# The sum of the two expert rows of row tiles 1 to 4 on GpSimd instead of VectorE

## The chip, the cores and the metric

The kernel runs on one core of a Trainium2 chip. The metric is the device time of one launch in microseconds (us); three runs of the kernel before gave 1686.21 to 1688.44, with a median of 1687.64. A core has TensorE (PE), VectorE (DVE), ScalarE (ACT), GpSimd (POOL) and SyncE (SP). All of them issue work in program order from a queue of their own, and wait for one another on semaphores. PE, DVE, ACT and POOL compute; here POOL and SP also issue the transfers between HBM and the on-chip memory (SBUF).

## The reference

A step of a two-layer (DEPTH = 2) transformer over 640 rows of 1024 numbers: 128 rows of a prompt and 512 latent rows. Each layer has attention and then a mixture of experts:

```python
sh1, sc1, gt1, sh2, sc2, gt2 = modulation(cond, lp['w_mod'], lp['b_mod'])
h = rms_norm(x, lp['g_norm1']) * (1 + sc1) + sh1
... # attention on h @ w_in, two branches, then
x = x + gt1 * mixed
h2 = rms_norm(x, lp['g_norm2']) * (1 + sc2) + sh2
x = x + gt2 * moe(h2, lp['w_router'], lp['b_router'], lp['w_gate'], lp['w_up'], lp['w_down'])
```

The mixture picks two experts for each row and adds their two outputs, each times its weight. What the change touches is the last line: the two weighted expert outputs of a row are added, multiplied by the gate `gt2` and added to `x`; and, in the next layer, the first line of the norm reads that `x`.

## The kernel before

The 640 rows are five row tiles of 128 (t = 0 is the prompt). All arithmetic is fp32; the large products are made of three passes over values that are split in a high and a low part (`hi`, `lo`). The engines' programs are written out by hand, in the order in which they run, with a semaphore (`Signal`) for each hand-over.

The mixture works on 18 tiles of gathered rows. Its outputs are scattered to a buffer in HBM (`ye_d`), the first and the second expert's row of each token in two halves. When the last tile has been stored, SP loads them back (`load_back`, L605 to L610): for each row tile t, `Y1[t]` and `Y2[t]`, 128 x 1024 fp32 or 512 KB each, and signals `gathered[t]`. The old `x` and the gate `gt` have been brought back earlier (`rows_return`, L590 to L601). Then VectorE does three operations for each row tile: the sum of the two rows (`mix_rows`, L1355), the gate (`gate_rows`, L1359) and the addition to `x` (`add_rows`, L1363), which signals `x_ready[t]`.

This happens at two places.

- **The change of layers**, at the start of layer 1. VectorE does row tile 0, and then in its loop over t: the mean square of tile t, the inverse root (L1319 to L1325), the three operations of tile t+1, half of the normed and modulated tile t read from PSUM (`head_half`, L1335), and the low part of it (`head_lo`, L1344). ScalarE squares `x` (`head_square`, L952), takes the root (L956), scales the row tile (`head_xn`, L960), and reads the other half from PSUM (`head_evac`, L966 to L972). TensorE transposes the scaled tile (L1800) in the middle of the projection of the tile before it (L1882 to L1884). `qk_evac` (L985, L986) takes the finished projection of a tile to SBUF, and VectorE sums its squares (`head_sum`, L1349).
- **The tail**, after layer 1: nothing is left but the five row tiles, three operations each, and SP stores each finished tile to `y_out` (L669).

GpSimd computes nothing in the kernel before. It issues transfers: in the mixture the indirect ones (rows of `xg`, weights of the experts, the stores to `ye_d`, L827), and at the change of layers one copy of `x` to HBM (L716), when `x_ready` of the last row tile has come.

Of the kernel before, what the change touches and what calls it, by code (L numbers as in the profile page):

```python
# [18 lines left out]
ALU = mybir.AluOpType  # L19
# [7 lines left out]
DEPTH = 2  # L27
NT = 5
# [109 lines left out]
def program(nc, w_stream, w_gu, w_dn, x_in, c_cols, params, b_mod2, vecs, g_norm2, da_kc, da_vc, na_kc, na_vc, na_bias,  # L138
# [3 lines left out]
    with ctx:  # L142
# [3 lines left out]
        def at(name, shape, dt, kb=None):  # L146

            size = int(np.prod(shape[1:])) * (2 if dt == BF16 else 4)
            if kb is None:
                off = top[0]  # L150
                top[0] += (size + 31) // 32 * 32
            else:
                off = area + int(kb * 1024)
                assert int(kb * 1024) + size <= AREA_KB * 1024, name
            return nc.alloc_sbuf_tensor_at(name, shape, dt, offset=off)

        def sem(name):
            return ctx.enter_context(nc.semaphore(name))
# [32 lines left out]
        tri = at("tri", [P, P], BF16)  # L191
# [71 lines left out]
        tri_f = at("tri_f", [P, P], F32, 48)  # L263
        x = at("x", [P, NT, D], F32, 0)
        gt = at("gt", [P, 2, D], F32, 20)
        Y1 = [at(f"y1_{t}", [P, D], F32, kb) for t, kb in enumerate((36, 74, 78, 82, 86))]
        Y2 = [at(f"y2_{t}", [P, D], F32, 50 + 4 * t) for t in range(NT)]
# [103 lines left out]
        s_zero = sem("zeros_ready")  # L371
# [1 line left out]
        s_cond = sem("cond_loaded")  # L373
        p_loaded = [sem(f"p_loaded{i}") for i in range(KC // 2)]
        p_used = sem("p_used")
        s_tri = sem("tri_cast")
        s_modini = sem("mod_bias")

        dve_chain = Signal("dve_chain", 0)
# [98 lines left out]
        y_dve = Signal("y_dve", MOE_TILES)  # L478
        y_stored = [Signal(f"y_stored{b}", half[b], 0, 16) for b in range(2)]
        gathered = [Signal(f"gathered{t}", 5 if t == 0 else 3, 0, 16) for t in range(NT)]  # L480
        x_ready = Signal("x_ready", NT)


# [190 lines left out]
        def _(po):  # L674
# [17 lines left out]
            for l in range(DEPTH):  # L692
# [11 lines left out]
                def load_vec(dst, which, cond, s):  # L704
                    po.dma_start(dst, mod_d[l, cond, which * D:(which + 1) * D].partition_broadcast(P)).then_inc(s.sem, 16)

                def norm_vecs():
# [3 lines left out]
                    for cond in range(2):  # L711
                        load_vec(sh[:, cond, :], 3, cond, shift_loaded)

                if l >= 1:
                    po.wait_ge(x_ready.sem, x_ready.at(l - 1, NT - 1))
                    po.dma_start(x_spill, x[:]).then_inc(x_spilled.sem, 16)  # L716

# [106 lines left out]
                def store_rows(n):  # L824
                    po.wait_ge(y_act.sem, y_act.at(l, n))
                    po.wait_ge(y_dve.sem, y_dve.at(l, n))
                    po.indirect_dma_start(ye_d, bass.IndirectOffsetOnAxis(row_i[:, XD_COL[n]:XD_COL[n] + 1], 0),  # L827
                                          ysb[n % 2][:], None, bounds_check=2 * NT * P - 1,
                                          oob_is_err=False).then_inc(y_stored[n % 2].sem, 16)
# [38 lines left out]
                store_rows(MOE_TILES - 2)  # L868
                store_rows(MOE_TILES - 1)

            po.wait_ge(x_parked.sem, x_parked.layer * DEPTH)
            for s in (kv_out, mod_stored, h2_stored, y_stored[0], y_stored[1], sg_stored[0], sg_stored[1]):
                po.wait_ge(s.sem, s.layer * DEPTH)
# [334 lines left out]
        def _(dve):  # L1208
# [4 lines left out]
            dve.wait_ge(s_const, 128)  # L1213
            dve.tensor_copy(rc[:], rc_f[:])
            dve.tensor_scalar(br_b[:], br_b[:], 0.5, None, ALU.add)
            dve.tensor_copy(tri[:], tri_f[:]).then_inc(s_tri, 1)
            steps = count()
            for l in range(DEPTH):

# [4 lines left out]
                def chained(ins):  # L1224
                    ins.then_inc(dve_chain.sem, 1)
                    return step()

                def after(n):
                    dve.wait_ge(dve_chain.sem, dve_chain.at(0, n))
# [121 lines left out]
                                      AX.X, ALU.add).then_inc(sum_ready.sem, 1)  # L1351

                def mix_rows(l, t):
                    dve.wait_ge(gathered[t].sem, gathered[t].at(l, gathered[t].n - 1))
                    after(chained(dve.tensor_tensor(Y1[t][:], Y1[t][:], Y2[t][:], ALU.add)))  # L1355

                def gate_rows(l, t):
                    mix_rows(l, t)
                    return chained(dve.tensor_tensor(Y1[t][:], Y1[t][:], gt[:, GI(t), :], ALU.mult))  # L1359
# [105 lines left out]
                for i in range(len(DA_UNITS) + 3):  # L1465
                    if 1 <= i <= len(DA_UNITS):
                        j = i - 1
                        t, h = DA_UNITS[j]
# [26 lines left out]
                    if i >= 3 and DA_UNITS[i - 3][1] == DA_HEADS - 1:  # L1495
                        t = DA_UNITS[i - 3][0]
# [290 lines left out]
        def _(pe):  # L1787
            def keep_busy(n, bank):
                for _ in range(n):
                    pe.matmul(ps[:, bank, 0:4 * HD], ident[:], rope_c[:].rearrange("p a b -> p (a b)"), start=True, stop=True)  # L1790
# [32 lines left out]
            keep_busy(2, 2)  # L1823
            head_columns(0)
            keep_busy(11, 2)
            pe.wait_ge(s_tri, 1)
            for l in range(DEPTH):

                def mod_pair(g, kc):
# [571 lines left out]
```

## Time and profile before

| | |
|---|---|
| three runs, median (lowest to highest) | 1687.64 us (1686.21 to 1688.44) |
| the profiled execution, own time | 1685.31 us |
| its span | 1683.5 us |
| PE busy | 1552.3 us, 92% |
| DVE busy | 899.7 us, 53% |
| ACT busy | 701.3 us, 42% |
| POOL busy | 296.0 us, 18% |

The span is what the records of the trace cover, the own time also what lies around it (1.8 us). Busy shares are means over stages with different limits. The change acts on two short stretches, 847 to 907 us and 1657 to 1683.5 us of the span, so those are read by themselves, in order of time.

### The profile page before, as it was taken

The page shows a single profiled execution, that of the slowest core. Times are in us where ns is not written, and L with a number is a line of the kernel's source. Part 1 is how long each engine was busy: PE and PEld are TensorE (multiplying, and loading weights), DVE is VectorE, ACT ScalarE, POOL GpSimd, SP SyncE. Part 2 cuts the span into 40 slices and gives each one's busy share as a digit, 9 for nine tenths or more (in the row PEclk, how much of TensorE's full clock was granted, in tenths as well). Part 3 has the DMA queues.
Part 4 walks back from the last instruction along what each step waited for, and adds up shares of the span by engine and source line. Part 5 has one row for each costly group of instructions (what it writes and reads, how often), then busy time and mean ns, then how long its engine had stood idle before and what let it go on. Part 6 is the DMA issues. An engine that isn't in the chain of part 4 may idle for free.

```text
span 1683.5 us, 21787 instructions
## 1 busy us (share of the span) xinstructions
PE 1552.3 (92%) x8180; PEld 1107.9 (66%) x8180; DVE 899.7 (53%) x1723; ACT 701.3 (42%) x1335; POOL 296.0 (18%) x321
## 2 busy tenths in 40 slices
PE   4999999999999989798869999999999999889992
PEld 1777777777787854454547777777778878555561
DVE  1576664445554744344575756553465556344554
ACT  4543554445522314344554455534554132134550
POOL 1000000011101015454200010000111010355540
PEclk9999999999999989999989999999999999999996
DMA  8541206534366289989635512354345253898747
GB/s 339 206 145 63 69 26 204 177 111 155 126 216 265 86 321 411 419 321 377 219 150 190 193 50 70 112 180 140 113 151 196 92 200 125 325 416 355 272 144 286
DMA packets 92376, 337.55 MB, mean 201 GB/s; under 512 B 20960, under 2 KB 21024, under 8 KB 89328
## 3 DMA queue, kind: packets, MB, share of 16 engines
q1 hardware_dynamic: 53136, 197.68, 32.3%
q0 software_dynamic: 38992, 135.86, 21.5%
q10 hardware_dynamic: 144, 2.62, 0.4%
q8 instruction: 65, 1.06, 0.3%
q14 instruction: 39, 0.32, 0.1%
HBM read 351.22 MB, written 47.35 MB: 237 GB/s over the span
## 4 chain that ended last, share of the span: by engine, by line
PE 82%; DMA 8%; DVE 5%; ACT 2%; issue 1%; SPq 1%; POOL 0%; POOLq 0%; ACTq 0%; DVEq 0%
PE ps L1882 17%; PE ps L1884 17%; PE ps L1883 17%; DMA dn_b<-w_dn,eidx 6%; PE ps L1874 5%; PE ps L2212 5%; PE ps L2261 4%; PE ps L2034 3%; PE ps L2016 2%; PE ps L1841 2%; PE ps L2094 2%; PE ps L2228 2%; PE ps L1790 1%; PE ps L2195 1%; PE ps L2068 1%
## 5 line engine op out<-in xcount | busy, mean ns | idle before, releaser
L1882 PE MATMUL ps<-hi,hT_hi 128*128 128x512 f32 x960 | 392.9, 409 | 5.5 <-ACT o_a L1092 3.0
L1884 PE MATMUL ps<-hi,hT_lo 128*128 128x512 f32 x960 | 376.8, 393 | 0.0
L1883 PE MATMUL ps<-lo,hT_hi 128*128 128x512 f32 x960 | 376.5, 392 | 0.0
L1882 PEld LDWEIGHTS ps<-hi,hT_hi 128*128 128x128 f32 x960 | 182.3, 190 | 63.8 <-issue 20.3
L1884 PEld LDWEIGHTS ps<-hi,hT_lo 128*128 128x128 f32 x960 | 181.3, 189 | 40.0
L1883 PEld LDWEIGHTS ps<-lo,hT_hi 128*128 128x128 f32 x960 | 182.2, 190 | 32.5
L888 ACT ACTIVATE hi<-raw 128x1024 fp32r<-128x1024 f32 x106 | 108.6, 1055 | 136.6 <-DMA raw<-w_stream 136.6
L1234 DVE TENSOR_TENSOR lo<-raw,hi 128x1024 fp32r<-128x1024 f32 x106 | 127.4, 1221 | 63.8 <-ACT hi L888 63.5
L1713 DVE TENSOR_TENSOR lo<-raw,hi 128x1024 fp32r<-128x1024 f32 x96 | 112.8, 1222 | 39.1 <-ACT hi L1159 39.1
L2212 PE MATMUL ps<-gu_a,xT 128*64 128x512 f32 x256 | 113.3, 595 | 0.0
L2212 PE MATMUL ps<-gu_b,xT 128*64 128x512 f32 x256 | 113.3, 595 | 0.0
L1159 ACT ACTIVATE hi<-raw 128x1024 fp32r<-128x1024 f32 x96 | 95.5, 1056 | 5.0 <-PE ps L1884 5.0
L2261 PE MATMUL ps<-dn_a,hidT 128*64 128x512 f32 x128 | 65.2, 657 | 24.9 <-DMA dn_b<-w_dn,eidx 23.3
L1069 ACT ACTIVATE e_da<-ps,neg_m 128x640 f32<-128x640 f32 (+1 forms) x80 | 56.0, 705 | 71.5 <-DVE neg_m L1491 71.4
L1491 DVE TENSOR_REDUCE neg_m<-ps 128x1 f32<-128x640 f32 (+1 forms) x80 | 53.7, 713 | 56.7 <-PE ps L2023 38.1
L1756 DVE TENSOR_TENSOR hid<-ps,silu_g 128x256 f32<-128x256 f32 x36 | 15.3, 425 | 118.0 <-ACT silu_g L1185 102.1
L2212 PEld LDWEIGHTS ps<-gu_a,xT 128*64 128x64 f32 x256 | 33.7, 137 | 66.7 <-issue 66.7
L1349 DVE TENSOR_REDUCE ssum<-sq 128x8 f32<-128x512 f32 x40 | 27.3, 685 | 79.2 <-ACT stg L986 79.2
L1176 ACT ACTIVATE ysb<-ps,w_slot 128x512 f32<-128x512 f32 x36 | 24.8, 689 | 107.6 <-PE ps L2261 61.5
L1730 DVE TENSOR_SCALAR ysb<-ps,w_slot 128x512 f32<-128x512 f32 x36 | 27.0, 751 | 77.8 <-PE ps L2261 43.4
L985 ACT ACTIVATE sq<-ps 128x512 f32<-128x512 f32 x40 | 24.0, 599 | 105.8 <-PE ps L1884 105.8
L1185 ACT ACTIVATE silu_g<-ps 128x256 f32<-128x256 f32 x36 | 13.8, 384 | 124.5 <-PE ps L1884 61.4
(312 smaller groups left out, 2917.6 us busy)
## 6 DMA issues: line engine op xcount, KB each, us to landing
raw<-w_stream SPq DMA_DIRECT2D x112, 512.0 KB
raw<-w_gu SPq DMA_DIRECT2D x80, 512.0 KB
raw_m<-w_stream SPq DMA_DIRECT2D x68, 512.0 KB, 5.6
raw<-w_dn SPq DMA_DIRECT2D x40, 512.0 KB
bias_na<-na_bias POOLq DMA_DIRECT2D x32, 384.0 KB, 3.3
sg<-sg_d POOLq DMA_DIRECT2D x8, 1280.0 KB, 9.1
y<-ye_d SPq DMA_DIRECT2D x20, 512.0 KB, 7.3
raw_p<-w_stream SPq DMA_DIRECT2D x16, 512.0 KB, 16.3
```

The lines of the kernel that those rows point to most:

```text
L888: act.activation(hi[s][:], raw[s][:], ACT.Copy).then_inc(is_hi.sem, 1)
L1069: act.activation(e_da[:, i % 2, m, 0:nk], ps_flat[:, m * 1024:m * 1024 + nk], ACT.Exp, bias=neg_m[:, 2 * (i % 2) + m:2 * (i % 2) + m + 1], ...
L1159: act.activation(hi[k][:], raw[w][:], ACT.Copy).then_inc(is_hi.sem, 1)
L1234: dve.tensor_tensor(lo[s][:], raw[s][:], hi[s][:].bitcast(F32), ALU.subtract).then_inc(is_lo.sem, 1)
L1491: dve.tensor_reduce(neg_m[:, c:c + 1], ps_flat[:, m * 1024:m * 1024 + nk], AX.X, ALU.max, negate=True).then_inc(mx_done.sem, 1)
L1713: dve.tensor_tensor(lo[w][:], raw[w][:], hi[k][:].bitcast(F32), ALU.subtract).then_inc(is_lo.sem, 1)
L1874: ins = pe.transpose(ps[:, 5 + n % 2, j * P:(j + 1) * P], src, ident[:])
L1882: pe.matmul(out, w_hi, m_hi, start=first, stop=False)
L1883: pe.matmul(out, w_hi, m_lo, start=False, stop=False)
L1884: return pe.matmul(out, w_lo, m_hi, start=False, stop=last)
L2212: ins = pe.matmul(ps[cs, 0, :], xT[:, kc, cs], pair_gu[q % 2][h][:, kc * 512:(kc + 1) * 512], start=(kc == 0), stop=(kc == KC - 1))
L2261: ins = pe.matmul(ps[cs, 2 + c, :], hidT[:, k, cs], pair_dn[q % 2][h][k][:, c * 512:(c + 1) * 512], start=(k == 0), stop=(k == 1))
```

## The change

GpSimd gets `sum_rows`, which waits for `gathered[t]` and adds `Y2[t]` to `Y1[t]` for t = 1 to 4; it stands ahead of its copy of `x` at the change of layers, and at the end of its program for the tail. VectorE's `mix_rows` keeps the sum of row tile 0, and for the others waits for GpSimd's signal `y_summed` and goes on with the gate and `x`. To have a semaphore for it, `s_tri` is given up, and the wait of TensorE for it at the start becomes a wait for the third count of `s_zero`, raised by the same instruction.

```diff
+        y_summed = Signal("y_summed", NT - 1)
...
+                def sum_rows(l):
+                    for t in range(1, NT):
+                        po.wait_ge(gathered[t].sem, gathered[t].at(l, gathered[t].n - 1))
+                        po.tensor_tensor(Y1[t][:], Y1[t][:], Y2[t][:], ALU.add).then_inc(y_summed.sem, 1)
+
                 if l >= 1:
+                    sum_rows(l - 1)
                     po.wait_ge(x_ready.sem, x_ready.at(l - 1, NT - 1))
                     po.dma_start(x_spill, x[:]).then_inc(x_spilled.sem, 16)
...
+            sum_rows(DEPTH - 1)
             po.wait_ge(x_parked.sem, x_parked.layer * DEPTH)
...
-            dve.tensor_copy(tri[:], tri_f[:]).then_inc(s_tri, 1)
+            dve.tensor_copy(tri[:], tri_f[:]).then_inc(s_zero, 1)
...
                 def mix_rows(l, t):
+                    if t >= 1:
+                        dve.wait_ge(y_summed.sem, y_summed.at(l, t - 1))
+                        return
                     dve.wait_ge(gathered[t].sem, gathered[t].at(l, gathered[t].n - 1))
                     after(chained(dve.tensor_tensor(Y1[t][:], Y1[t][:], Y2[t][:], ALU.add)))
...
-            pe.wait_ge(s_tri, 1)
+            pe.wait_ge(s_zero, 3)
```

Line numbers differ in the changed kernel: the sum, the gate and the addition to `x` on VectorE are L1365, L1369 and L1373 there, the sum on GpSimd is L717, the copy of `x` L722, the store to `ye_d` L833. GpSimd's queue at the change of layers, before (`y_1_152` is `Y1[1]`, `y_1_157` is `Y2[1]`):

```order
L827 DMA ye_d<-ysb_251,row_i 1280x1024
L827 DMA ye_d<-ysb_93,row_i 1280x1024
L716 DMA x_spill<-x 128x5120
L721 DMA kT<-da_kc 128x4x128
L722 DMA v<-da_vc 128x512
```

and GpSimd's queue at the same place now:

```order
L833 DMA ye_d<-ysb_251,row_i 1280x1024
L833 DMA ye_d<-ysb_93,row_i 1280x1024
L717 ISA
L717 TENSOR_TENSOR y_1_152<-y_1_152,y_1_157 128x1024
L717 TENSOR_TENSOR y_2_153<-y_2_153,y_2_158 128x1024
L717 TENSOR_TENSOR y_3_154<-y_3_154,y_3_159 128x1024
L717 TENSOR_TENSOR y_4_155<-y_4_155,y_4_160 128x1024
L722 DMA x_spill<-x 128x5120
```

Four sums stand ahead of the copy of `x`, and in front of the first of them an instruction `ISA` without operands, which the build adds and which waits for nothing. The tail's four sums have no such row.

VectorE's queue at the change of layers, before, from the end of the last split of weights:

```order
L1238 TENSOR_TENSOR lo_65<-raw_64,hi_66 128x1024
L1355 TENSOR_TENSOR y_0_151<-y_0_151,y_0_156 128x1024
L1359 TENSOR_TENSOR y_0_151<-y_0_151,gt 128x1024
L1363 TENSOR_TENSOR x<-x,y_0_151 128x1024
L1313 TENSOR_SCALAR nv<-xss 128x1
L1319 RECIPROCAL n_114<-n_114 128x1
L1320 SCALAR_TENSOR_TENSOR nr<-n_114,nv 128x1
L1322 TENSOR_SCALAR nr<-nr 128x1
L1325 TENSOR_TENSOR nr<-nr,n_114 128x1
L1355 TENSOR_TENSOR y_1_152<-y_1_152,y_1_157 128x1024
L1359 TENSOR_TENSOR y_1_152<-y_1_152,gt 128x1024
L1363 TENSOR_TENSOR x<-x,y_1_152 128x1024
```

and VectorE's queue there now, from the inverse root of row tile 0:

```order
L1326 RECIPROCAL n_114<-n_114 128x1
L1327 SCALAR_TENSOR_TENSOR nr<-n_114,nv 128x1
L1329 TENSOR_SCALAR nr<-nr 128x1
L1332 TENSOR_TENSOR nr<-nr,n_114 128x1
L1369 TENSOR_TENSOR y_1_152<-y_1_152,gt 128x1024
L1373 TENSOR_TENSOR x<-x,y_1_152 128x1024
L1342 TENSOR_SCALAR y_0_151<-ps,mT 128x128 x4
L1351 TENSOR_TENSOR hT_lo<-y_0_151,hT_hi 128x4x128 x2
```

Each of the row tiles 1 to 4 has lost its first 128 x 1024 operation on VectorE; everything else stands in the order of before. In the tail the same four operations are gone from VectorE's 15.

## Rows read from the trace of the kernel before

**Rows 1.** Timeline of DVE, change of layers: start us, us, engine, line, op [idle <-releaser]

```profile
847.54 1.23 DVE L1355 TENSOR_TENSOR y<-y,y 128x1024 f32<-128x1024 f32 x1 [2.55 <-DMA y<-ye_d]
...
850.06 1.23 DVE L1363 TENSOR_TENSOR x<-x,y 128x1024 f32<-128x1024 f32 x1
...
853.18 0.22 DVE L1320 SCALAR_TENSOR_TENSOR nr<-n,nv 128x1 f32<-128x1 f32 x1
...
853.70 1.22 DVE L1355 TENSOR_TENSOR y<-y,y 128x1024 f32<-128x1024 f32 x1
...
856.21 1.23 DVE L1363 TENSOR_TENSOR x<-x,y 128x1024 f32<-128x1024 f32 x1
857.35 1.36 DVE L1335 TENSOR_SCALAR y<-ps,mT 128x128 f32<-128x128 f32 x4
...
865.25 1.36 DVE L1335 TENSOR_SCALAR y<-ps,mT 128x128 f32<-128x128 f32 x4
```

**Rows 2.** Timeline of ACT, change of layers

```profile
853.82 1.15 ACT L960 ACTIVATE y<-x,nr 128x1024 f32<-128x1024 f32 x1 [0.87 <-DVE nr L1325]
...
858.75 0.63 ACT L972 ACTIVATE hT_hi<-y 128x512 fp32r<-128x512 f32 x1 [0.87 <-DVE y L1335]
859.28 1.04 ACT L952 ACTIVATE y<-x 128x1024 f32<-128x1024 f32 x1
...
868.64 0.58 ACT L985 ACTIVATE sq<-ps 128x512 f32<-128x512 f32 x1
```

**Rows 3.** Timeline of PE, change of layers

```profile
860.15 0.50 PE L1882 MATMUL ps<-hi,hT_hi 128*128 128x512 f32 x1 [1.88 <-DVE hT_lo L1344]
...
862.91 1.09 PE L1800 MATMUL ps<-ident,y 128*128 128x128 f32 x8 [1.08 <-ACT y L960]
```

**Rows 4.** Chain that ended last, one turn of it: start us, us, what

```profile
879.24 0.60 ACT sq L985
...
880.35 0.69 DVE ssum L1349
...
882.99 1.97 PE ps L1800 x8
...
889.84 0.60 ACT sq L985
```

**Rows 5.** Timeline of DVE and of SP's queue, tail

```profile
1662.14 1.22 DVE L1355 TENSOR_TENSOR y<-y,y 128x1024 f32<-128x1024 f32 x1 [7.88 <-DMA y<-ye_d]
...
1665.91 14.95 SPq L669 DMA_DIRECT2D y_out<-x  x5
...
1679.28 1.23 DVE L1363 TENSOR_TENSOR x<-x,y 128x1024 f32<-128x1024 f32 x1
```

**Rows 6.** Line L610, issue and landing of the ten loads: change of layers

```profile
L610 SPq DMA_DIRECT2D y<-ye_d x10: 326/444/807, 842.7 to 847.3; - x10
...
DMA to landing us min/median/max: 3.4/7.3/11.1
```

**Rows 7.** The same line in the tail

```profile
L610 SPq DMA_DIRECT2D y<-ye_d x10: 319/446/809, 1657.3 to 1662.0; - x10
...
DMA to landing us min/median/max: 3.5/7.3/12.6
```

**Rows 8.** Timeline of POOL, last store, and three issues within the mixture

```profile
840.53 0.97 POOL L827 DMA_INDIRECT ye_d<-ysb,row_i  x1 [4.33 <-DVE ysb L1730]
...
1604.85 1.00 POOL L792 DMA_INDIRECT xg<-h_d,inv_i  x1 [3.37 <-PE ps L2195]
1606.16 1.67 POOL L801 DMA_INDIRECT gu_b<-w_gu,eidx  x1 [0.30 <-issue]
...
1612.06 1.95 POOL L808 DMA_INDIRECT dn_a<-w_dn,eidx  x1 [0.31 <-issue]
```

**Rows 9.** Timeline of DVE around those three issues

```profile
1605.74 1.23 DVE L1713 TENSOR_TENSOR lo<-raw,hi 128x1024 fp32r<-128x1024 f32 x1 [1.66 <-ACT hi L1159]
...
1609.64 5.77 DVE L1713 TENSOR_TENSOR lo<-raw,hi 128x1024 fp32r<-128x1024 f32 x5 [0.52 <-ACT hi L1159]
```

**Rows 10.** All of line L1713: duration ns min/median/max, first and last start us

```profile
L1713 DVE TENSOR_TENSOR lo<-raw,hi x96: 1217/1220/1227, 644.6 to 1640.6; 128x1024 fp32r<-128x1024 f32 x96
```

More of the change, by code:

```diff
@@ L375, in program @@
         p_used = sem("p_used")
-        s_tri = sem("tri_cast")
         s_modini = sem("mod_bias")
```

## The prediction

> **What bounds the kernel now.** I read the page first: TensorE is busy for 92% of the span and makes most of the chain, so an operation taken from VectorE can only pay where TensorE waits. Then I read, in order of time, the two stretches in which VectorE's row operations stand: the change of layers and the tail.
>
> At the change of layers the loads of the expert rows end the wait at 847.54, and VectorE does the three operations of row tile 0, the last from 850.06 to 851.3 [rows 1]. ScalarE squares it, VectorE makes the inverse root (L1320 at 853.18), ScalarE scales the tile at 853.82 [rows 1, 2]. VectorE then does the three operations of row tile 1, at a spacing of 1.26 us, from 853.70 to 857.4, and only then reads row tile 0 back from PSUM, at 857.35, though the transposes had long been done; ScalarE's L972 waits 0.87 us for that and its square of tile 1 follows at 859.28; TensorE starts its projection at 860.15 after a wait for VectorE's L1344 [rows 1 to 3]. The transposes of tile 1 come at 862.91 [rows 3], and the first projection is taken out at 868.64 [rows 2]. From here on the chain turns once in 10.6 us (879.24 to 889.84): the evacuation, the small sum L1349, the scaling, the transposes, three units of matmuls [rows 4]. None of VectorE's row operations is in that turn. So VectorE's operations bound something for row tiles 0 and 1 only.
>
> In the tail VectorE is alone: first operation at 1662.14, last one ending at 1680.5, then one store [rows 5]. Fifteen operations, five tiles of 1.26 + 1.26 + 1.14 = 3.66 us.
>
> **When the data come.** The ten loads are issued by 847.3, and the slowest lands 11.1 us after its issue, so the last row tile is there at 858.4; the first is there at 847.5. Between them lie four tiles, 2.7 us each: tiles 1 to 4 at about 850.2, 853, 855.7, 858.4 [rows 1, 6]. In the tail the last one is at 1662.0 + 12.6 = 1674.6 and the first at 1662.1, so 3.1 us each at most: I take 1665.2, 1668.3, 1671.5, 1674.6 [rows 5, 7].
>
> **What a sum costs on GpSimd.** No row shows GpSimd computing. Below, it can be no faster than VectorE with the same shape, 1.22 us [rows 1]. ScalarE reads one operand of this shape in 1.15 us [rows 2]; two read one after the other make 2.30, and a third pass for the result 3.45, the upper end. I take 2.30 us: it is the plain case of an engine that takes its two operands in turn, and it lies in the middle of the bounds. The Trainium skill's page "GPSIMD Engine Reference" (section 3.1) gives 4497 ns for 2048 fp32 numbers and says that the two inputs share one read port; by it the sum would be near 2.3 us as well. No row here shows it.
>
> **Do the two engines disturb each other?** This decides the sign. In the mixture GpSimd's issue of an indirect transfer takes 1.00 us at 1604.85, when VectorE is idle. At 1606.16 it takes 1.67 us; VectorE's L1713, two operands from SBUF, runs until 1606.97. At 1612.06 it takes 1.95 us, within five such operations back to back [rows 8, 9]. So GpSimd is held up by 0.7 to 0.95 us, about until the running operation of VectorE ends, and then gets on although a further one is queued. VectorE's L1713 shows nothing of it: 96 of them within 1217 to 1227 ns [rows 10]. One direction is thus seen, with a GpSimd instruction that touches little memory; the other, VectorE held up by a GpSimd instruction that reads two whole tiles, has no row. Bounds: nothing, or the whole length of the GpSimd sum for each VectorE operation with two SBUF operands that meets one. I take the second, since the rows show a wait of whole operations and not a slight slowing.
>
> The rule that speaks against this change is in the Trainium skill, page "SBUF — State Buffer", section "Who interferes with whom": a VectorE instruction with two SBUF inputs and a GpSimd instruction that reads SBUF exclude each other, and the second to issue blocks until the first is done. Rows 8 and 9 agree with it for VectorE first and GpSimd second. By that rule all four sums and all of VectorE's row operations have to run one after the other, as in my forecast; without it the first rival holds.
>
> **The tail, with exclusion.** VectorE ends row tile 0 at 1665.9. From there 4 sums x 2.30 = 9.2 us and 4 x (1.26 + 1.14) = 9.6 us of gates and additions share one door, in whatever order: end at 1684.7 instead of 1680.5. The stores and the landings (last at 1674.6) do not bind. **+4.2 us.**
>
> **The change of layers, with exclusion.** Sum 1 has its data at about 850.2 to 851 and gets in after the addition of tile 0: 851.3 to 853.6. L1320 (two operands) waits from 853.18 to 853.6; sum 2 gets in behind it, 853.7 to 856.0, and L1325 waits for it, so the scaling of tile 0 starts at 856.3 instead of 853.82: 2.5 us late. Now it matters who goes first when both wait. If they alternate: sum 3 until 858.4, gate 1 until 859.6, sum 4 until 862.0, addition 1 until 863.2, and L1335 starts there instead of at 857.35, 5.9 late. If VectorE goes on: gate and addition of tile 1 until 858.7, L1335 is 1.4 us late, but sum 3 and sum 4 then meet L1344 and the inverse root of tile 1, and the transposes of tile 1 come 3.6 us late instead. Behind that the shorter queue for tile 2 gives 0.6 us back (the take-out at 868.64 waited for ScalarE, which was held by L1335 at 865.25 [rows 1, 2]). That makes +5.3 or +3.0; I take the middle, **+4.1 us**. From there on the turn of rows 4 passes it on unchanged.
>
> **The rest.** The removed operations themselves: 1.26 us x 4 at each place, already counted. GpSimd's queue: behind the four sums stands only the copy of `x`, which waits for the last `x_ready` anyhow; its sums are done by then. In the tail nothing stands behind them but final waits. The `ISA` row before the first sum waits for nothing, and GpSimd is free from 841.5 [rows 8] until the first data at 850 to 851: up to 9 us of it are hidden, at nothing; above that each us delays tile 1. The Trainium skill's "GPSIMD Engine Reference" (section 2.1) speaks of about 6 us for the first call of newly loaded code; by it the row would be hidden, and no row here shows one. The semaphore change at the start raises the same count by the same instruction: nothing.
>
> **Sum.** 4.2 + 4.1 = +8.3 us. The profiled execution took 1685.31 us (1683.5 of span and 1.8 around it), so 1693.6 on its scale. It lies 2.3 us under the median of the three runs; on the median's scale that is 1695.9. I say 1695.5.
>
> **The rivals.**
>
> 1. *VectorE is not held up.* Then L1335 of tile 0 needs no third operation before it and starts 1.1 to 1.2 us earlier, ScalarE's L972 and the square of tile 1 follow 0.9 earlier, and for tile 1 ScalarE is ready before the matmuls end, so that the take-out of 868.64 comes 1.7 us earlier. In the tail the last tile is 1674.6 + 2.3 + 0.1 + 2.4 = 1679.4 instead of 1680.5: 1.1 less. Together -2.8 us, 1684.8 by the median. For it: VectorE's constant 1.22 us in rows 10. Against it: GpSimd's stretched issues. Even here the gain of 16 us of VectorE's work is mostly not to be had, because tiles 2 to 4 hang on another chain. Chance 0.25.
> 2. *They share more finely, or the sum holds the door for less than it lasts.* With 1.22 to 1.7 us for each sum, the tail comes to -0.1 to +1.8 and the change of layers to 0 to +1.4: together within -0.1 and +3.2, 1687.5 to 1690.8. For it: an issue that waits still gets on at the next boundary, with VectorE unslowed. Chance 0.15.
> 3. *The sum takes the upper end, 3.45 us, or the `ISA` row lasts well over 9 us.* At 3.45 us, 4 x 1.15 more in the tail (+8.8) and twice as many lost at the change of layers (+7 to +10): about +17, 1705. Against it: it needs three separate passes. Chance 0.05.
> 4. *The change of layers gains nothing and loses nothing, because something else ends that stretch.* Speaking against it: the trace has a wait of TensorE for VectorE there, 1.88 us [rows 3]. It would leave +4.2. I count it with the forecast.
>
> **How the numbers follow.** Forecast (exclusion, 2 to 2.5 us per sum, +6 to +10): 0.55. Its own range is 1693 to 1698.5. What a measurement can tell from no change is about 0.2% of the time, 3.4 us. Rival 1 lies within that (-2.8), with a small chance of more: if GpSimd took 1.7 us, the tail would gain 1.6 and the sum be -3.4. Faster by over 0.2%: 0.04. Within: 0.21 of rival 1 and most of rival 2, with little of the forecast: 0.35. Slower by over 0.2%: 0.61. The range that holds 8 in 10 has to take in most of rival 1 on the one side and alternation at every meeting on the other: 1684.8 to 1699.5.
>
> **What would show it.** In the changed profile: GpSimd rows L717 of about 2.3 us, eight of them; if exclusion holds, VectorE's L1369 and L1373 either last over 2 us or start late beside a sum, L1332 of row tile 0 ends near 856, and the last L1373 ends about 22 us after the first L1365 of the tail, where it was 18.4. If L1369 and L1373 keep 1.22 us beside the sums, rival 1 has won. A steady 10.6 us turn for row tiles 2 to 4 shows that nothing was to be won there. What would make the forecast wrong: a sum much shorter than 2 us, or VectorE unhindered.

## The result and the profile after

The changed kernel takes 1692.77 us (median of 14 runs, 1687.81 to 1697.04), the kernel before 1686.53 us (14 runs, 1682.18 to 1690.92). The ratio is 1.0033, with a 95% interval of 1.0023 to 1.0044: +5.6 us (3.9 to 7.4). The whole interval lies above 1, so the changed kernel is slower, by a third of a per cent. The forecast was 1695.5 us, from a sum of +8.3.

The page of the profile after, its span and its busy times:

```profile
span 1691.6 us, 21789 instructions
...
PE 1555.1 (92%) x8180; PEld 1109.7 (66%) x8180; DVE 901.5 (53%) x1715; ACT 700.5 (41%) x1335; POOL 318.9 (19%) x329
```

VectorE has eight instructions of 1.22 us fewer (1715; it had 1723) and is busy for 901.5 us where it was 899.7. The work is gone and the busy time is not. The trace books the time for which an instruction is held as part of its duration, so the page hides what happened; the timelines show it.

GpSimd's sums, first the groups of line L717 in the changed kernel (duration ns min/median/max, first and last start), then its timeline at the two places (start us, us, engine, line, op, idle before and releaser); they answer to [rows 8]:

```profile
L717 POOL TENSOR_TENSOR y<-y,y x8: 2327/3008/3397, 852.1 to 1678.2; 128x1024 f32<-128x1024 f32 x8
L717 POOLq MODIFY_POOL_CONFIG  x2: 39/39/39, 841.4 to 841.4; - x2
```

```profile
852.09 11.71 POOL L717 TENSOR_TENSOR y<-y,y 128x1024 f32<-128x1024 f32 x4 [10.70 <-DMA y<-ye_d]
...
1669.83 11.64 POOL L717 TENSOR_TENSOR y<-y,y 128x1024 f32<-128x1024 f32 x4 [9.07 <-DMA y<-ye_d]
```

An undisturbed sum takes 2.33 us, and two of the eight do. The other six take 2.76 to 3.40, because GpSimd too waits, for the operation that VectorE is in. The `ISA` row of the order appears as an instruction of 39 ns at 841.4, and the first sum waits for its data until 852.09, so nothing of it is on the path.

VectorE at the change of layers, in the changed kernel (answers to [rows 1]):

```profile
848.89 1.23 DVE L1365 TENSOR_TENSOR y<-y,y 128x1024 f32<-128x1024 f32 x1 [2.79 <-DMA y<-ye_d]
...
853.91 0.15 DVE L1320 TENSOR_SCALAR nv<-xss 128x1 f32<-128x1 f32 x1 [1.28 <-ACT y L959]
...
854.53 0.34 DVE L1327 SCALAR_TENSOR_TENSOR nr<-n,nv 128x1 f32<-128x1 f32 x1
...
855.09 2.08 DVE L1332 TENSOR_TENSOR nr<-nr,n 128x1 f32<-128x1 f32 x1
857.09 1.21 DVE L1369 TENSOR_TENSOR y<-y,gt 128x1024 f32<-128x1024 f32 x1
858.34 3.26 DVE L1373 TENSOR_TENSOR x<-x,y 128x1024 f32<-128x1024 f32 x1
861.52 1.35 DVE L1342 TENSOR_SCALAR y<-ps,mT 128x128 f32<-128x128 f32 x4
862.79 2.16 DVE L1351 TENSOR_TENSOR hT_lo<-y,hT_hi 128x512 fp32r<-128x512 f32 x2
```

L1332 works on one number per partition. It takes 0.16 us alone and 2.08 here, beside the second sum. L1373 takes 3.26 instead of 1.22, beside the third. L1369 between them runs free. L1342 starts 12.63 us after the first row operation, where it was 9.81 [rows 1]. That is +2.82, and the rows give it: 1.92 + 2.04 us of holding and 0.12 at L1327 make 4.08, less 1.26 for the sum that VectorE no longer does.

The fourth sum (860.47 to 863.80) falls on L1342 and L1351. L1342 keeps its time. L1351, which has two SBUF operands, lasts 2.16 us for its two halves; in the kernel before it was

```profile
858.62 1.48 DVE L1344 TENSOR_TENSOR hT_lo<-y,hT_hi 128x512 fp32r<-128x512 f32 x2
```

That is another 0.7 us of holding, and TensorE waits for this operation (answers to [rows 3]):

```profile
865.01 0.50 PE L1892 MATMUL ps<-hi,hT_hi 128*128 128x512 f32 x1 [1.67 <-DVE hT_lo L1351]
...
867.33 1.09 PE L1810 MATMUL ps<-ident,y 128*128 128x128 f32 x8 [0.65 <-ACT y L967]
```

Counted from VectorE's first row operation, the first projection starts 3.5 us late (16.12 against 12.61) and the transposes of row tile 1 start 3.1 us late (18.44 against 15.37).

ScalarE in the changed kernel, the scaling of row tile 0 and the first take-out of a projection (answers to [rows 2]):

```profile
857.20 1.15 ACT L967 ACTIVATE y<-x,nr 128x1024 f32<-128x1024 f32 x1 [2.90 <-DVE nr L1332]
...
872.58 0.60 ACT L992 ACTIVATE sq<-ps 128x512 f32<-128x512 f32 x1 [0.40 <-PE ps L1894]
```

From VectorE's first row operation to the scaling it is 8.31 us, before 6.28. To the take-out it is 23.69, before 21.10 [rows 1, 2]: +2.6.

VectorE in the tail of the changed kernel (answers to [rows 5]):

```profile
1666.67 1.22 DVE L1365 TENSOR_TENSOR y<-y,y 128x1024 f32<-128x1024 f32 x1 [7.74 <-DMA y<-ye_d]
...
1672.64 3.35 DVE L1369 TENSOR_TENSOR y<-y,gt 128x1024 f32<-128x1024 f32 x1 [2.23 <-POOL y L717]
1676.02 3.25 DVE L1373 TENSOR_TENSOR x<-x,y 128x1024 f32<-128x1024 f32 x1
1679.19 3.36 DVE L1369 TENSOR_TENSOR y<-y,gt 128x1024 f32<-128x1024 f32 x1
1682.58 1.22 DVE L1373 TENSOR_TENSOR x<-x,y 128x1024 f32<-128x1024 f32 x1
...
1687.38 1.23 DVE L1373 TENSOR_TENSOR x<-x,y 128x1024 f32<-128x1024 f32 x1
```

Sum, operation, sum, operation: VectorE and GpSimd take turns. The tail lasts 21.94 us from the first start to the last end and lasted 18.37 [rows 5], +3.6. The parts: a wait of 2.23 for the first sum, three operations held by some 2.1 each (6.3), less four removed sums of 1.25 (5.0).

The two profiled spans differ by 8.1 us. Start to the first row operation +1.35 (848.89 against 847.54), take-out of row tile 3 at the change of layers +1.0, the unchanged code between the two places +2.2, the tail +3.6, the end equal. So the two places account for 4.6, and 3.5 are differences of stretches that the edit doesn't touch.

### The profile page after: what moved, and what is told of

It is laid out like the page before. It is cut to its first block, busy times and chain, and to the rows that moved or that the text cites. A ratio compares the mean times of both kernels' runs of the same rounds, so it can differ in the third digit from the quotient of the medians.

```text
span 1691.6 us, 21789 instructions
## 1 busy us (share of the span) xinstructions
PE 1555.1 (92%) x8180; PEld 1109.7 (66%) x8180; DVE 901.5 (53%) x1715; ACT 700.5 (41%) x1335; POOL 318.9 (19%) x329
## 4 chain that ended last, share of the span: by engine, by line
PE 81%; DMA 10%; DVE 5%; ACT 1%; issue 1%; SPq 1%; POOL 0%; POOLq 0%; ACTq 0%; DVEq 0%
PE ps L1892 17%; PE ps L1894 16%; PE ps L1893 16%; DMA dn_b<-w_dn,eidx 6%; PE ps L1884 5%; PE ps L2222 5%; PE ps L2271 4%; PE ps L2044 3%; PE ps L2026 2%; PE ps L1851 2%; PE ps L1800 2%; PE ps L2104 2%; PE ps L2238 2%; DMA raw_m<-w_stream 2%; PE ps L2205 1%
## 5 line engine op out<-in xcount | busy, mean ns | idle before, releaser
L2271 PE MATMUL ps<-dn_b,hidT 128*64 128x512 f32 x128 | 66.3, 667 | 0.0
```

The lines of the kernel that those rows point to most:

```text
L2271: ins = pe.matmul(ps[cs, 2 + c, :], hidT[:, k, cs], pair_dn[q % 2][h][k][:, c * 512:(c + 1) * 512], start=(k == 0), stop=(k == 1))
```

## Where the change of layers gives back 1.6 us

The first take-out is 2.6 us late, the fourth only 1.0. The chain of waits of the changed kernel, in order of time (start us, us, what), holds the turn of [rows 4] twice, with different lengths:

```profile
872.58 0.60 ACT sq L992
...
876.33 1.97 PE ps L1810 x8
878.30 0.43 PE ps L1892
...
883.06 0.60 ACT sq L992
...
886.81 1.09 PE ps L1810 x8
887.90 0.23 PE ps L1892
...
892.04 0.60 ACT sq L992
```

The turn from 872.58 takes 10.48 us, the next one 8.98. The difference is TensorE's clock. Busy time by stretch (stretch, us, busy us and count of PE, PEld, DVE, ACT, POOL; then the granted clock, DMA share, GB/s), of the changed kernel and then of the kernel before:

```profile
876.00:879.00 3.00, 2.67 (x11) 2.48 (x12) 2.12 (x5) 1.78 (x5) 0.00 (x0) 0.51 0.00 0
879.30:896.30 17.00, 12.15 (x59) 9.58 (x58) 9.64 (x24) 10.59 (x20) 0.61 (x1) 0.99 0.36 154
```

```profile
872.80:876.20 3.40, 3.40 (x13) 2.92 (x11) 3.37 (x7) 2.24 (x6) 0.00 (x0) 0.50 0.00 0
876.20:883.00 6.80, 4.37 (x20) 3.26 (x19) 3.82 (x10) 4.01 (x7) 0.00 (x0) 1.00 0.00 0
883.00:886.40 3.40, 3.40 (x12) 3.08 (x13) 3.37 (x6) 2.14 (x5) 0.60 (x1) 0.50 0.00 0
```

A granted clock of 0.50 is TensorE's lower level, 1.2 GHz, 1.0 the upper, 2.4 GHz. Before, TensorE pauses at the start of each turn, and the transposes behind the pause run at the lower level (0.50 from 872.80 to 876.20, and again from 883.00 to 886.40): 1.97 us for the eight of them, 0.43 us for a step of the chain behind them, a turn of 10.6. In the changed kernel one of three turns keeps the upper level through its transposes: 1.09 and 0.23, 8.98 in all. Its pause is as long as that of the turn before it, 2.43 us each, so the length of the pause doesn't tell the two apart. A delay at the start of this stretch thus isn't passed on one to one. Which turns are spared differs from kernel to kernel and, as `ride_copy` shows below, also where the code of this stretch is the same. The cause of that choice stays open.

## The experiments

The theory was the forecast's: a VectorE operation with two SBUF operands and a GpSimd instruction that reads SBUF exclude each other. The rivals: GpSimd's sums delay through their results alone (VectorE waits for them), or only certain sums matter. In the kernels that move sums to GpSimd, `ON_POOL` lists their row tiles by layer (tiles 1 to 4 in both would be the changed kernel), and the rest of the edit is this:

```diff
+                    for t in ON_POOL[l]:
+                        po.wait_ge(gathered[t].sem, gathered[t].at(l, gathered[t].n - 1))
+                        po.tensor_tensor(Y1[t][:], Y1[t][:], Y2[t][:], ALU.add).then_inc(y_summed.sem, 1)
...
+                    if t in ON_POOL[l]:
+                        dve.wait_ge(y_summed.sem, len(ON_POOL[0]) * l + ON_POOL[l].index(t) + 1)
+                        return
```

### The tail alone

```diff
+ON_POOL = {0: (), 1: (1, 2, 3, 4)}
```

> GpSimd's sums are kept in the tail alone; the change of layers is as in the kernel before. Theory A (the two engines exclude each other while GpSimd sums): from the start of VectorE's first row operation of the tail to the end of its last one 21.9 us, as in the changed kernel, against 18.4 before; +3.5 us, ratio about 1.002. VectorE's operations beside a sum last 2 to 3.4 us. Theory B (no exclusion, VectorE only waits for the sum of its row tile and the sum is slow): VectorE keeps 1.22 us per operation and the stretch is at most 0.5 us off 18.4. If the loss of the changed kernel sits in the change of layers alone, this one is level with the kernel before.

Measured: 1689.24 us (12 runs), ratio 1.0019 (1.0006 to 1.0033), that is +3.2 us (1.0 to 5.6). The tail lasts 21.94 us in its profile, as in the changed kernel, and the take-outs at the change of layers stand within 0.2 us of where they stood before (21.10, 31.70, 42.32 and 52.91 us after the first row operation). The tail is the larger and the steadier part of the loss.

### The change of layers alone

```diff
+ON_POOL = {0: (1, 2, 3, 4), 1: ()}
```

> GpSimd's sums are kept at the change of layers alone; the tail is as in the kernel before. Theory A: the first projection is taken out (ScalarE's square of it) 23.7 us after VectorE's first row operation, against 21.1 before: +2.6 us; the last one +1 to +2.6, the difference being turns in which TensorE keeps its full clock at the transposes; ratio 1.0005 to 1.0015. Together with the run that keeps the tail's sums it adds up to the changed kernel's 1.0033. Theory B: 1.7 us less than before at the first take-out, ratio 0.999.

Measured: 1688.62 us (12 runs), ratio 1.0010 (0.9997 to 1.0023), +1.7 us (-0.5 to +3.9). VectorE reads row tile 0 from PSUM 12.63 us after its first row operation, exactly as in the changed kernel. The first take-out is 2.6 us late (23.68) and the fourth 0.7 us early (52.05), since two turns of this profile are of the short kind; the expectation had it 1 to 2.6 us late. By the time alone this part can't be told from nothing; that the start of the stretch is late is read from the profile. The two parts, +0.19% and +0.10%, make up the whole, +0.33%, within their intervals.

### GpSimd reads a tile twice for nobody

The kernel before, with four sums into buffers that nobody reads, when the rows of a tile have landed. VectorE does all its own work and waits for none of them.

```diff
+            spare = [G[:, 0, :], G[:, 1, :]] + [r[:].rearrange("p a b -> p (a b)") for r in raw_h[1]]
+            for t in range(1, NT):
+                po.wait_ge(gathered[t].sem, gathered[t].at(DEPTH - 1, gathered[t].n - 1))
+                po.tensor_tensor(spare[t - 1], Y2[t][:], Y2[t][:], ALU.add)
```

> The kernel before, with VectorE's fifteen tail operations unchanged; beside them GpSimd does four additions of two 128x1024 operands into spare memory, each when the loads of row tile 1 to 4 have landed. VectorE waits for none of them. Theory A: each addition holds VectorE for its 2.3 us whenever both want to run, so the tail stretch grows from 18.4 to 25 to 27.6 us, and single operations of VectorE last up to 3.4 us. Theory B: 18.4 us, since nothing waits for GpSimd.

Measured: one run, 1692.39 us. The tail of its profile lasts 24.90 us, +6.5. Timeline of GpSimd, and of VectorE:

```profile
1665.50 5.51 POOL L874 TENSOR_TENSOR G<-y 128x1024 f32<-128x1024 f32 x2 [8.88 <-DMA y<-ye_d]
```

```profile
1665.21 1.22 DVE L1367 TENSOR_TENSOR x<-x,y 128x1024 f32<-128x1024 f32 x1
1666.36 2.91 DVE L1359 TENSOR_TENSOR y<-y,y 128x1024 f32<-128x1024 f32 x1
1669.30 2.80 DVE L1363 TENSOR_TENSOR y<-y,gt 128x1024 f32<-128x1024 f32 x1
```

Four operations of VectorE last 2.80 to 2.91 us and the eleven others 1.22 or 1.23. Nothing waits for a result here, so this settles the mechanism: GpSimd's instruction itself holds VectorE, one operation per sum, by 1.6 to 1.7 us. The expectation had 2.3 us for each and 25 to 27.6 us for the tail. The sum is shorter when both operands are the same tile: the second one here ends 1.7 us after the VectorE operation for which it waited (1671.01 against 1669.27). In the changed kernel it is 2.2 us, from 1675.99, the end of L1369, to the end of this one:

```profile
1674.87 3.32 POOL L717 TENSOR_TENSOR y<-y,y 128x1024 f32<-128x1024 f32 x1
```

### GpSimd reads one tile for nobody

```diff
-                po.tensor_tensor(spare[t - 1], Y2[t][:], Y2[t][:], ALU.add)
+                po.tensor_copy(spare[t - 1], Y2[t][:])
```

> As the kernel before, with four GpSimd copies of one 128x1024 operand into spare memory beside VectorE's tail, at the landing of row tiles 1 to 4; nothing waits for them. If any GpSimd instruction that reads from SBUF excludes VectorE's two-operand operations, the tail stretch grows by the length of the four copies (1 to 3.5 us each; 4 to 14 us in all). If only GpSimd's second read stream does, it stays at 18.4 us.

Measured: one run, 1692.42 us; the tail lasts 21.59 us, +3.2. Timeline of GpSimd, and of VectorE:

```profile
1669.56 1.07 POOL L874 COPY G<-y 128x1024 f32<-128x1024 f32 x1 [9.60 <-DMA y<-ye_d]
1672.03 1.84 POOL L874 COPY G<-y 128x1024 f32<-128x1024 f32 x1 [1.40 <-DMA y<-ye_d]
```

```profile
1669.65 2.06 DVE L1359 TENSOR_TENSOR y<-y,y 128x1024 f32<-128x1024 f32 x1
1671.74 1.23 DVE L1363 TENSOR_TENSOR y<-y,gt 128x1024 f32<-128x1024 f32 x1
1673.00 1.94 DVE L1367 TENSOR_TENSOR x<-x,y 128x1024 f32<-128x1024 f32 x1
```

One read stream is enough. The copy at 1669.56 holds the VectorE operation that starts 0.09 us after it by 0.84 us. The copy at 1672.03 meets one that began at 1671.74, waits for it itself (1.84 instead of 1.07 us) and then holds the next one. Four copies, four held operations of 1.94 to 2.06 us.

This run also shows how much of a single time comes from the turns. Its code at the change of layers is that of before, and its first take-out comes 23.18 us after the first row operation instead of 21.10, beside a stretch from 861.4 to 868.3 in which the granted clock is 0.51 (1.00 in the kernel before). That is 2.1 us without any edit there. The +3.2 of the tail is read from the tail; the single time is not used.

### GpSimd writes one tile for nobody

```diff
-                po.tensor_copy(spare[t - 1], Y2[t][:])
+                po.memset(spare[t - 1], 0.0)
```

> As the kernel before, with four GpSimd fills (128x1024, write only) of spare memory beside VectorE's tail, at the landing of row tiles 1 to 4. If it is reading that excludes, the tail stretch stays at 18.4 us and no operation of VectorE lasts over 1.3 us. If any use of SBUF by GpSimd excludes, it grows by the length of the fills, about 1 us each.

Measured: one run, 1689.87 us; the tail lasts 18.35 us, as before (18.37). A row of GpSimd, and the VectorE operation that starts 0.10 us before it with the one behind:

```profile
1669.33 0.95 POOL L874 MEMSET G<- 128x1024 f32 x1 [8.61 <-DMA y<-ye_d]
```

```profile
1669.23 1.22 DVE L1367 TENSOR_TENSOR x<-x,y 128x1024 f32<-128x1024 f32 x1
1670.38 1.22 DVE L1359 TENSOR_TENSOR y<-y,y 128x1024 f32<-128x1024 f32 x1
```

All four fills take 0.95 us and no operation of VectorE exceeds 1.23. Each fill began inside a VectorE operation with two SBUF operands and didn't wait for it, as the copies and sums do. So it is reading that excludes. One case didn't occur: no VectorE operation began before a fill was all but over. That a fill doesn't hold a VectorE operation that comes second is argued and not shown.

### One sum in VectorE's pause

```diff
+ON_POOL = {0: (1,), 1: ()}
```

> GpSimd sums row tile 1 at the change of layers and nothing else. Theory A: the sum falls mostly in VectorE's pause after the addition of row tile 0 (about 1.9 us), holds up the inverse root by 0.4 us or less, and takes 1.25 us from VectorE before it reads row tile 0 from PSUM: the first take-out comes 0.6 to 1 us earlier than the 21.1 us of before. If GpSimd's sum costs as such, wherever it lies, it comes later.

Measured: one run, 1686.86 us, which tells nothing by itself. GpSimd's sum runs from 850.06 for 2.43 us, mostly in the pause in which VectorE waits for ScalarE's square. The only trace of it on VectorE is L1328 with 0.34 instead of 0.22 us. VectorE reads row tile 0 from PSUM 8.80 us after its first operation (9.81 before) and the first take-out comes at 20.23 (21.10): 0.9 us earlier. Sum 1 of the changed kernel was thus no loss; sums 2 to 4 were.

### Only the sums that nobody waits for early

```diff
+ON_POOL = {0: (2, 3, 4), 1: ()}
```

> At the change of layers GpSimd sums row tiles 2, 3 and 4, and VectorE sums tiles 0 and 1 itself; the tail is as before. None of GpSimd's three sums is waited for at row tile 0 or 1. Theory A: they still hold VectorE's operations there, as the data of tile 2 land while it makes the inverse root of tile 0: VectorE reads row tile 0 from PSUM 12.5 to 16.5 us after its first row operation, against 9.8 in the kernel before and 12.6 in the changed one. Theory B (only waits for y_summed cost): 9.8 us, as before, since these sums are needed later.

Measured: one run, 1692.74 us. Row tile 0 is read from PSUM at 15.79 us after the first operation (before 9.81), and the first take-out comes at 26.59 (21.10), +5.5. Timeline of VectorE, and of GpSimd:

```profile
852.78 0.16 DVE L1327 RECIPROCAL n<-n 128x1 f32<-128x1 f32 x1 [0.27 <-ACT n L964]
852.98 2.01 DVE L1328 SCALAR_TENSOR_TENSOR nr<-n,nv 128x1 f32<-128x1 f32 x1
...
855.22 2.31 DVE L1333 TENSOR_TENSOR nr<-nr,n 128x1 f32<-128x1 f32 x1
...
858.70 3.26 DVE L1370 TENSOR_TENSOR y<-y,gt 128x1024 f32<-128x1024 f32 x1
```

```profile
852.64 2.34 POOL L718 TENSOR_TENSOR y<-y,y 128x1024 f32<-128x1024 f32 x1 [11.29 <-DMA y<-ye_d]
```

Three sums, three held operations (1.8 + 2.15 + 2.04 = 6.0 us), and the same 6.0 us between 9.81 and 15.79. Until then VectorE has used no result of GpSimd. The sums of the tiles that are needed last do more harm alone than all four together: 15.79 against 12.63. Of the 3.16 us, 1.25 are the sum of row tile 1, which VectorE does itself here, and 1.9 are more holding, since two of the sums now fall on the inverse root of tile 0.

### One sum in the tail

```diff
+ON_POOL = {0: (), 1: (4,)}
```

> GpSimd sums row tile 4 in the tail and nothing else. Its data land 12.5 us after VectorE's first operation, when VectorE is at row tile 3. Theory A: one sum of 2.3 us replaces 1.25 us on the shared way, the tail stretch is 18.4 + 1.1 = 19.5 us, and one operation of VectorE lasts 2 to 3.4 us. Theory B: 18.4 - 1.25 = 17.1 us, since the sum is done (12.5 + 2.4 = 14.9 us) before VectorE needs it at 14.7 to 14.9.

Measured: one run, 1688.12 us; the tail lasts 19.12 us, +0.75. A single VectorE operation is held, L1370 at 1675.68 with 3.24 us: 2.02 lost, 1.25 won by the removed sum. One moved sum that meets one operation costs the difference. (The expectation had 19.5, with 2.3 us of holding.)

### TensorE makes sums with the identity

The other engine that could make the sums is TensorE: it has little or no work of its own at these places, and its results lie in PSUM. It gets row tile 1 at the change of layers, row tiles 2 and 3 in the tail. At the change of layers four of the eight idle matmuls ahead of the first transposes go:

```diff
+ON_PE = {0: {1: 2}, 1: {2: 2, 3: 5}}
...
+                    if t in ON_PE[l]:
+                        dve.wait_ge(y_summed.sem, len(ON_PE[0]) * l + sorted(ON_PE[l]).index(t) + 1)
+                        b = 512 * ON_PE[l][t]
+                        return chained(dve.tensor_tensor(Y1[t][:], ps_flat[:, b:b + D], gt[:, GI(t), :], ALU.mult))
...
+                for c in range(2):
+                    for j, y in enumerate((Y1[t], Y2[t])):
+                        ins = pe.matmul(ps[:, ON_PE[l][t] + c, :], ident[:], y[:, 512 * c:512 * c + 512], start=(j == 0), stop=(j == 1))
...
+                    keep_busy(30, 4)
+                    pe.wait_ge(gathered[0].sem, gathered[0].at(l, gathered[0].n - 1))
+                    keep_busy(20, 4)
```

> No sum on GpSimd. TensorE adds the two rows by products with the identity into PSUM: row tile 1 at the change of layers, row tiles 2 and 3 in the tail (where idle matmuls keep its clock up); VectorE reads the sum from PSUM in its gate operation and does the other tiles with three operations. Theory A: what failed in the changed kernel is GpSimd's share of VectorE's way to SBUF, not the moving of the sum; TensorE and PSUM do not share it, so VectorE's operations stay at 1.2 to 1.3 us and the tail stretch falls from 18.4 to 16.0 us; at the change of layers the first take-out comes 0.5 to 1.7 us earlier. Sum -2.5 to -4 us, ratio 0.998. Theory C (handing over the sum costs as much as it saves, whoever makes it): level, 1.000. If TensorE runs at its lower clock in the tail its two sums take 3.4 us each and the tail gains nothing.

Measured: 1692.97 us (8 runs), ratio 1.0037 (1.0023 to 1.0051). The expectation missed: it had a gain, and a tail of 16.0 us; the tail lasts 25.5. Timeline of TensorE, and of VectorE, in the tail:

```profile
1654.59 21.85 PE L1795 MATMUL ps<-rope_c,ident 128*128 128x256 f32 x100
1676.28 7.03 PE L1801 MATMUL ps<-y,ident 128*128 128x512 f32 x16
```

```profile
1679.91 1.23 DVE L1362 TENSOR_TENSOR y<-ps,gt 128x1024 f32<-128x1024 f32 x1 [8.54 <-PE ps L1801]
```

The 50 idle matmuls of `keep_busy` are 100 records and take 21.85 us, 0.44 for a matmul and 0.22 for a record, so the sums began only at 1676.28 and VectorE waited 8.54 us for them. A sum of a row tile takes 3.5 us (7.03 for two). The expectation had such a time for the lower clock alone; the granted clock is 1.00 from 1655 to 1684. At the change of layers VectorE reads row tile 0 from PSUM 0.1 us earlier (9.73), but the first take-out comes at 23.08 instead of 21.10, 2.0 us late. As in `ride_copy`, a stretch that ran at 1.00 before has the lower clock here in most of its length:

```profile
861.00:868.00 7.00, 6.56 (x22) 5.57 (x23) 5.51 (x10) 4.39 (x10) 0.00 (x0) 0.58 0.01 2
```

Whether the removed idle matmuls have a part in that wasn't tried. VectorE's gate with an operand in PSUM keeps its 1.23 us.

### The two small ones together

The sum of row tile 1 on GpSimd at the change of layers, that of row tile 3 on TensorE in the tail, with fewer idle matmuls:

```diff
+ON_PE = {0: {}, 1: {3: 2}}
+ON_POOL = {0: (1,), 1: ()}
...
+                    keep_busy(20, 4)
+                    pe.wait_ge(gathered[0].sem, gathered[0].at(l, gathered[0].n - 1))
+                    keep_busy(15, 4)
+                    pe_sum(l, 3)
```

> Of the sums, GpSimd does the one of row tile 1 at the change of layers alone, in VectorE's pause, and TensorE does the one of row tile 3 in the tail, by products with the identity into PSUM, kept at its full clock by idle matmuls that end before the data land. Theory A (what costs is running beside VectorE's two-operand operations, not the hand-over): VectorE reads row tile 0 from PSUM 0.9 us earlier after its first row operation than the 9.8 us of before; in the tail TensorE's sum takes 3.5 us from the landing 8.5 us after VectorE's first operation and is done at 12.0, VectorE is ready at 11.0, no operation of VectorE lasts over 1.3 us, and the stretch is 18.1 us against 18.4. Together -1.2 us, ratio 0.9993, less than five rounds can tell from 1. Theory C (the hand-over itself costs): at or above 18.4 us and 9.8 us.

Measured: 1683.45 us (12 runs) against 1685.39 (17 runs), ratio 0.9993 (0.9980 to 1.0006). It isn't distinguishable from the kernel before. Row tile 0 is read from PSUM 1.0 us earlier (8.82 instead of 9.81), but the tail is no shorter (18.51 against 18.37; the expectation had 18.1). VectorE waits for TensorE's sum:

```profile
1675.57 1.23 DVE L1373 TENSOR_TENSOR y<-ps,gt 128x1024 f32<-128x1024 f32 x1 [1.31 <-PE ps L1812]
```

It started at 1671.83, when its rows had landed, and took 3.70 us. The removed sum gave 1.25 and the wait took 1.31. No version tried here beats the kernel before by an amount that could be measured.

## Why the prediction was right, by its steps

**The total.** The direction and the mechanism were right, the sum of +8.3 too high: measured +5.6 (3.9 to 7.4), and the forecast's own band began at +6. The two places give 4.6 in the profile, and 3.2 and 1.7 in the kernels that change one of them. Of the 2.7 us between 1695.5 and 1692.77, 1.1 belong to the base: the median of three runs was 1687.64, that of fourteen is 1686.53.

**What bounds.** Right: nothing was won outside the start of the change of layers and the tail. With one sum moved into a pause the gain at the first take-out was 0.9 us; rival 1 had 1.7 there, for all four sums moved and none disturbing.

**The price of a sum.** Right: 2.33 us where I took 2.30. I had doubled ScalarE's time for one operand. GpSimd's own copy of one operand takes 1.07 us (`ride_copy`), so the doubling fits, but no row had shown it, and that it came out so closely is in part luck.

**Exclusion.** Right, and shown by `ride_two`, `ride_copy` and `ride_memset` without any wait for a result. The rule of the Trainium skill, page "SBUF — State Buffer", section "Who interferes with whom", holds here in both directions: VectorE's 1.22 us become 3.25 to 3.36 beside a sum, and GpSimd's 2.33 us become up to 3.40 beside an operation of VectorE. Rival 1 (VectorE isn't held up) falls. Rival 2 (shorter hold) falls for the changed kernel: a VectorE operation beside a sum of 2.33 us loses 1.9 to 2.1. In `ride_two` it was 1.6 to 1.7 us, where the sum that reads one tile twice is itself shorter.

**The tail, +4.2.** Mechanism right, size a little off: +3.6 in the profile, +3.2 by the times. The order at the door was as forecast: four sums and eight operations one after the other, from the end of row tile 0 on. What was too high is the share of a sum. It lasts 2.33 us but takes only about 2.1 from VectorE: VectorE waited 2.23 us for the first, and the other three held an operation by 2.13, 2.03 and 2.14. That makes 8.5 us where I had 4 x 2.30 = 9.2; less the 5.0 of the removed sums it is +3.5. The rows of tile 1 landed 3.16 us after VectorE's first start (3.1 in the forecast), so the data were not what bound.

**The change of layers, +4.1.** The mis-sized term: +2.6 at the first take-out, of which +1.0 is left at the fourth. The first half of the error is the order at the door. I had averaged full alternation (+5.3) with VectorE going on (+3.0). What came is a mixture: L1332 is so short that the gate of tile 1 got through right behind it, the third sum then met the addition (L1373), and the fourth met L1351, as in the second variant. The read of row tile 0 from PSUM was 2.8 us late, where the variants had 5.9 and 1.4; the transposes of tile 1 were 3.1 us late, where the second had 3.6; and the take-out's +2.6 stands close to its +3.0. The forecast of the scaling was 2.5 us late, it was 2.0. The second half is a sentence that was wrong: "From there on the turn of rows 4 passes it on unchanged." The turn is 10.6 us only where its transposes meet the lower clock, and 9.0 where they don't. That the give-back comes from this is read from the traces, in which turn length and granted clock go together; no run here sets the clock, so it isn't shown by an experiment. A first take-out 2.1 us late in `ride_copy`, without an edit at that place, speaks for it.

**The rest at nothing.** Right: the `ISA` row is 39 ns long and 10.7 us ahead of the first landing.

## What to carry to other kernels

Moving elementwise work on SBUF from VectorE to GpSimd relieves VectorE only where VectorE pauses. Beside a busy VectorE each moved operation costs nearly its own length on GpSimd, less what was removed, and it costs VectorE time even when nobody waits for it: here about 2.1 us of holding stand against 1.25 of saving. Before moving anything, lay the new instruction's time on VectorE's timeline and count which operations it meets, the one-number ones of an inverse root included. The share of busy time can't answer this, since held time counts as busy.

## What the runs showed of the chip

- A GpSimd instruction with a single SBUF operand holds VectorE too (copy of 1.07 us, held by 0.7 to 0.84 us). One that only writes held nothing and wasn't held (four fills of 0.95 us).
- VectorE instructions with one tensor operand seem to be free. In `change_234` the reciprocal at 852.78 keeps its 0.16 us within GpSimd's sum from 852.64 to 854.98, and the next instruction, with two, takes 2.01. The same reciprocal keeps 0.16 within the sum of `change_tile1` (at 851.97). In the changed kernel L1342, which reads PSUM, keeps 1.35 us (before 1.36) beside the fourth sum, and L1351 right behind it, with two operands in SBUF, is held. No run was made for these alone.
- The two engines take turns when both always have something ready: GpSimd's sums grow to 3.2 to 3.4 us (most of a VectorE operation of 1.2 us in each), VectorE's operations to 3.25 to 3.36.
- An idle fp32 matmul of 256 columns on TensorE is two records and takes 0.44 us at a granted clock of 1.00. An fp32 sum of two 128x1024 tiles with the identity takes 3.5 to 3.7 us, longer than on GpSimd (2.33).
